# The mean of squares of a head as four 64x64 products, half of the squares made by GpSimd

## The reference

```
def rmsnorm(x, g):
    y = x32 * lax.rsqrt(jnp.mean(x32 * x32, axis=-1, keepdims=True) + NORM_EPS)
    return y * g

q = rmsnorm(split_heads(q, NSA_HEADS), q_g)          # HEAD_DIM = 64
o_slc = nsa_selected(q, rmsnorm(ks, k_g[1]), vs, importance)
o_win = nsa_window(q, rmsnorm(kw, k_g[2]), vw)
q = rmsnorm(split_heads(q, FOX_HEADS), q_g)          # in fox_group
k = rmsnorm(split_heads(k, FOX_HEADS), k_g)
```

## Time and profile before

| | |
|---|---|
| median of 3 runs | 443.76 us (443.74 to 444.36) |
| profiled execution, its own time | 444.42 us |
| its span | 442.5 us |
| granted clock of PE, mean over the span | 0.992 |
| PE, DVE, ACT, POOL busy | 96%, 66%, 59%, 18% of the span |
| chain that ended last, by engine | PE 81%, DVE 10%, ACT 4% |

### The profile page before, as it was taken

The page is one execution under the profiler, slowest core; times in us unless marked ns, Lnnn a source line. Parts: engine busy times, 40 slices in busy tenths (PEclk is TensorE's granted clock), DMA queues, the critical chain, the costliest instruction groups (busy, mean ns, idle before and its releaser), DMA issues.

```text
span 442.5 us, 6412 instructions
## 1 busy us (share of the span) xinstructions
PE 425.2 (96%) x2173; PEld 327.7 (74%) x2173; DVE 291.8 (66%) x609; ACT 262.6 (59%) x510; POOL 78.7 (18%) x129
## 2 busy tenths in 40 slices
PE   5799999999989899999999999999799999999997
PEld 1477788778978666676777987978577678888875
DVE  5976698867798877676158846788977268522204
ACT  4736885766776888877268878742687454311100
POOL 3302420000000275666000010000365200000000
PEclk9899999999999999999999999999899999999999
DMA  7831342342142200000012233642300014722005
GB/s 248 343 101 49 114 126 83 100 115 95 49 142 60 85 1 2 2 1 1 1 48 96 95 96 118 169 142 76 116 1 1 1 48 154 277 101 87 0 0 192
DMA packets 12961, 39.15 MB, mean 88 GB/s; under 512 B 1792, under 2 KB 2048, under 8 KB 12672
## 3 DMA queue, kind: packets, MB, share of 16 engines
q1 hardware_dynamic: 12928, 38.73, 26.8%
HBM read 32.43 MB, written 2.10 MB: 78 GB/s over the span
## 4 chain that ended last, share of the span: by engine, by line
PE 81%; DVE 10%; ACT 4%; issue 3%; DMA 2%; SPq 1%; POOL 0%; DVEq 0%; ACTq 0%
PE bank L1255 11%; PE bank L1257 11%; PE bank L1256 11%; PE bank L1369 7%; PE bank L1350 6%; PE bank L1470 5%; PE bank L1471 5%; PE bank L1469 5%; PE bank L1341 3%; PE bank L1342 3%; PE bank L1266 2%; PE bank L1236 2%; PE bank L1238 2%; PE bank L1237 2%; DMA x_raw<-in_xT 2%
## 5 line engine op out<-in xcount | busy, mean ns | idle before, releaser
L1255 PE MATMUL bank<-xh,wh 128*128 128x512 f32 x256 | 108.4, 423 | 0.3 <-DVE wl L883 0.3
L1257 PE MATMUL bank<-xh,wl 128*128 128x512 f32 x256 | 100.9, 394 | 0.0
L1256 PE MATMUL bank<-xl,wh 128*128 128x512 f32 x256 | 100.2, 391 | 0.0
L883 DVE TENSOR_TENSOR wl<-raw,wh 128x1024 fp32r<-128x1024 f32 (+1 forms) x51 | 61.2, 1204 | 34.7 <-ACT wh L551 34.4
L551 ACT ACTIVATE wh<-raw 128x1024 fp32r<-128x1024 f32 (+1 forms) x51 | 52.3, 1037 | 30.6 <-PE bank L1471 26.8
L1255 PEld LDWEIGHTS bank<-xh,wh 128*128 128x128 f32 x256 | 48.5, 189 | 14.0 <-issue 4.9
L1256 PEld LDWEIGHTS bank<-xl,wh 128*128 128x128 f32 x256 | 48.3, 189 | 13.6 <-issue 3.9
L1257 PEld LDWEIGHTS bank<-xh,wl 128*128 128x128 f32 x256 | 48.3, 188 | 10.9
L1078 DVE CUSTOM_DVE_ANT_0 bank<-bank,mask_row 128x256 f32<-128x256 f32 (+3 forms) x96 | 46.8, 500 | 13.6 <-PE bank L1342 13.0
L511 POOL TENSOR_SCALAR probs<-probs,rcp,gates 128x384 f32<-128x384 f32 (+3 forms) x44 | 27.2, 629 | 103.3 <-DVE rcp L1094 103.3
L1471 PE MATMUL bank<-wh,yl 128*128 128x512 f32 x96 | 37.8, 394 | 0.0
(11 more groups left out here) (213 smaller groups left out, 783.6 us busy)
## 6 DMA issues: line engine op xcount, KB each, us to landing
raw<-in_w_in SPq DMA_DIRECT2D x36, 512.0 KB, 3.3
raw<-in_w_out SPq DMA_DIRECT2D x12, 512.0 KB, 3.3
x_raw<-in_xT SPq DMA_DIRECT2D x8, 256.0 KB, 6.1
x_res<-in_x_tok SPq DMA_DIRECT2D x1, 2048.0 KB, 10.4
out_y<-y_out SPq DMA_DIRECT2D x8, 256.0 KB, 2.1
raw<-in_w_in SPq DMA_DIRECT2D x3, 384.0 KB, 3.1
cmp_w_sb<-in_cmp_w SPq DMA_DIRECT2D x1, 1024.0 KB, 10.1
kh_fox<-kh_fox SPq DMA_DIRECT2D x8, 128.0 KB, 2.3
```

The lines of the kernel that those rows point to most:

```text
L883: dve.tensor_tensor(wl[:, c % HL, cols], raw[:, c % RAW, cols], wh[:, c % HL, cols].bitcast(F32), ALU.subtract).then_inc(wl_ready, 1)
L1255: pe.matmul(dst, hi, xh[:, k, :], start=(k == 0), stop=False)
L1256: pe.matmul(dst, hi, xl[:, k, :], start=False, stop=False)
L1257: mm = pe.matmul(dst, lo, xh[:, k, :], start=False, stop=(k == KT - 1))
```

## The change

Each head mean is now four matmuls of 64 partitions by 64 result rows and 256 tokens, instead of one of 128 by 128 and 512 tokens. Tokens 0 to 255 use the two diagonal blocks. For tokens 256 to 511 the squares of a head lie on the other half of the partitions, so that their products use the two off-diagonal quarters of the array, and their results land on the head's own half again. These late squares are made by POOL (`swapped_squares`, two instructions of 64x256, from one half of the partitions to the other), ACT squares the early half only. Results of early tokens go to bank 4, of late tokens to bank 5 (`HEAD_MEAN`, quarters 0 and 3 of the two banks, which are now one tensor), and `NORM_W` has quarters 1 and 2. Since both banks are now written by the head mean, PE waits for the earlier chunk's `normed`, no longer for `norm_seed`, and for both POOL squares. POOL's program has the squares of `ks` to `nq` 3 before the probabilities of the first attention, those of `fq` 0 to `fk` 3 behind them, and the last `scale_input` between `fk` 0 and `fk` 1.

```diff
--- before.py
+++ after.py
@@ -191,10 +191,14 @@
             x_res = sb("x_res", [P, NT, D], F32, v)
             y_out = sb("y_out", [P, NT, D], F32, v)
 
-        bank = [ctx.enter_context(nc.psum_tensor(f"bank{i}", [P, SEQ], F32)) for i in range(8)]
+        banks = [ctx.enter_context(nc.psum_tensor(f"bank{i}", [P, SEQ], F32)) for i in range(4)]
+        norm_banks = ctx.enter_context(nc.psum_tensor("norm_banks", [P, 2 * SEQ], F32))
+        bank = ([b[:, :] for b in banks] + [norm_banks[:, 0:SEQ], norm_banks[:, SEQ:2 * SEQ]]
+                + [ctx.enter_context(nc.psum_tensor(f"bank{i}", [P, SEQ], F32))[:, :] for i in (6, 7)])
         PROJ = (bank[6], bank[0], bank[1])
         AUX_A, AUX_B, MEAN = bank[2], bank[3], bank[4]
-        NORM_W = bank[5]
+        quarters = norm_banks[:, :].rearrange("p (b c) -> p b c", b=4)
+        HEAD_MEAN, NORM_W = quarters[:, 0::3, :], quarters[:, 1:3, :]
         SCORE = (bank[4], bank[5], bank[6], bank[0])
         PT = (bank[7], bank[1])
         PTB = len(PT)
@@ -227,7 +231,7 @@
         cmp_evac, cmp_sq, cmp_mean, cmp_std = sem("cmp_evac"), sem("cmp_sq"), sem("cmp_mean"), sem("cmp_std")
         k_cmp_n, k_cmp_hr, k_cmp_ready = sem("k_cmp_n"), sem("k_cmp_hr"), sem("k_cmp_ready")
         v_cmp_T, v_cmp_ready = sem("v_cmp_T"), sem("v_cmp_ready")
-        sq_ready, norm_mean, norm_seed = sem("sq_ready"), sem("norm_mean"), sem("norm_seed")
+        sq_ready, sq_swapped, norm_mean, norm_seed = sem("sq_ready"), sem("sq_swapped"), sem("norm_mean"), sem("norm_seed")
         normed, h_ready, l_ready, stacked = sem("normed"), sem("h_ready"), sem("l_ready"), sem("stacked")
         cmp_s, cmp_shift, cmp_exp, cmp_p = sem("cmp_s"), sem("cmp_shift"), sem("cmp_exp"), sem("cmp_p")
         cmp_pT, cmp_pT_sb, cmp_o, cmp_o_read = sem("cmp_pT"), sem("cmp_pT_sb"), sem("cmp_o"), sem("cmp_o_read")
@@ -277,6 +281,9 @@
 
         def pool_square(k):
             return (sq, work, std)[POOL_SQUARES.index(k)][:, :]
+
+        def early_late(ap):
+            return ap.rearrange("p (b c) -> p b c", b=2)
 
         def half_of(s):
             return slice(s * HD, (s + 1) * HD)
@@ -523,14 +530,32 @@
                 pool.wait_ge(lru_ix, j + 1)
                 nc.gpsimd.tensor_tensor(ig[j][:, :], ig[j][:, :], u_pad[j][:, 0:SEQ], ALU.mult).then_inc(lru_ixs, 1)
 
+            def swapped_squares(c):
+
+                n = nth_normed(c)
+                pool.wait_ge(proj_read, proj_units(c) + 1)
+                if n >= 1:
+                    pool.wait_ge(norm_mean, n)
+                for s in range(2):
+                    x = qr[half_of(s), n % 2, SEQ // 2:]
+                    nc.gpsimd.tensor_tensor(sq[half_of(1 - s), SEQ // 2:], x, x, ALU.mult).then_inc(sq_swapped, 1)
+                pool.wait_ge(sq_swapped, 2 * n + 2)
+
             for j in range(LRU_T - 1):
                 gate_input(j)
             for j in range(LRU_T - 1):
                 scale_input(j)
             gate_input(LRU_T - 1)
-            pool.wait_ge(gates_ready, 1)
-            scale_probs(0, NSA_UNITS)
-            scale_input(LRU_T - 1)
+            pool.wait_ge(lru_ix, LRU_T)
+            for c in NORMED:
+                if c == AT["fq", 0]:
+                    pool.wait_ge(gates_ready, 1)
+                    scale_probs(0, NSA_UNITS)
+                    pool.wait_ge(p_scaled, NSA_UNITS)
+                if c == AT["fk", 1]:
+                    scale_input(LRU_T - 1)
+                    pool.wait_ge(lru_ixs, LRU_T)
+                swapped_squares(c)
             scale_probs(NSA_UNITS, UNITS)
 
 
@@ -582,7 +607,7 @@
                     n = nth_normed(c)
                     if n >= 1:
                         act.wait_ge(norm_mean, n)
-                    act.activation(sq[:, :], qr[:, n % 2, :], ACT.Square).then_inc(sq_ready, 1)
+                    act.activation(sq[:, 0:SEQ // 2], qr[:, n % 2, 0:SEQ // 2], ACT.Square).then_inc(sq_ready, 1)
 
             def after(c):
 
@@ -607,8 +632,8 @@
                     eighth = kind in ("nq", "fq")
                     if n >= 1:
                         act.wait_ge(normed, n)
-                    rsqrt_seed(MEAN[:, :], 64.0 if eighth else 1.0, std[:, :], work[:, :],
-                               NORM_W[:, :]).then_inc(norm_seed, 1)
+                    rsqrt_seed(HEAD_MEAN, 64.0 if eighth else 1.0, early_late(std[:, :]), early_late(work[:, :]),
+                               NORM_W).then_inc(norm_seed, 1)
 
             def norm_high(c):
 
@@ -899,7 +924,8 @@
                 if c in NORMED:
                     n = nth_normed(c)
                     dve.wait_ge(norm_seed, n + 1)
-                    link(dve.tensor_tensor(work[:, :], work[:, :], NORM_W[:, :], ALU.mult))
+                    w = early_late(work[:, :])
+                    link(dve.tensor_tensor(w, w, NORM_W, ALU.mult))
                     link(dve.scalar_tensor_tensor(std[:, :], work[:, :], 1.5, std[:, :], ALU.add, ALU.mult))
                     dve.scalar_tensor_tensor(qr[:, n % 2, :], qr[:, n % 2, :], ch(GAIN[kind]), std[:, :], ALU.mult,
                                              ALU.mult).then_inc(normed, 1)
@@ -1261,9 +1287,15 @@
 
                 n = nth_normed(c)
                 pe.wait_ge(sq_ready, n + 1)
+                pe.wait_ge(sq_swapped, 2 * n + 2)
                 if n >= 1:
-                    pe.wait_ge(norm_seed, n)
-                pe.matmul(MEAN[:, :], block_mean, sq[:, :], start=True, stop=True).then_inc(norm_mean, 1)
+                    pe.wait_ge(normed, n)
+                for b in range(2):
+                    for s in range(2):
+                        rows, dst = half_of(s), half_of(s if b == 0 else 1 - s)
+                        mm = pe.matmul(HEAD_MEAN[dst, b, :], block_mean[rows, rows], early_late(sq[:, :])[rows, b, :],
+                                       start=True, stop=True)
+                mm.then_inc(norm_mean, 1)
 
             def gates_of(j):
                 pe.wait_ge(conv_done, j + 1)
```

## The result

| | before | after |
|---|---|---|
| median | 443.75 us (443.21 to 444.36, 6 runs) | 448.69 us (447.13 to 451.43, 6 runs) |
| ratio, 95% interval | | 1.0107 (1.0085 to 1.0129) |
| profiled execution, its own time | 444.42 us | 451.43 us |
| its span, mean granted clock | 442.5 us, 0.992 | 449.4 us, 0.987 |

The change makes the kernel 4.9 us slower, where 3.25 were forecast. The profiled execution is the slowest of its six, so places are read from it and totals from the medians. In the kernel with the change the names move: L885 is the evacuation (L860 before), L908 the split of weights (L883), L928 to L930 the normalisation (L902 to L904), L541 POOL's squares, L1281 to L1283 the projection, L1296 the head mean.

What follows compares the result with a forecast made beforehand. PE, with 81% of the chain, was taken to bound the kernel. Products -1.4, `ks` +1.75, `fk` 1 +1.3, `fk` 0 and `fk` 3 +1.0, `nq` 3 +0.1, others +0.5: +3.25, median 447.0 us, between 444.7 and 449.9.

Steps and rivals of the forecast that it cites:

- The products: Fourteen head means on PE: each costs 0.69 to 0.80 us in place of 0.85, gaining 0.10 per call, -1.4 us together.
- Rival 1: At the head means: products of the two row halves do not run together, about 455 us; chance 1 in 10.
- rival 3: At the head means: shape changes for free when four quarters load together, 442.4 us; counted in 13 in 100 with rival 2.
- POOL's squares: On POOL: one half-width square takes 0.63 us, two 1.25, handovers about 0.1; hidden unless POOL and DVE hold each other up.
- The lock: POOL and DVE hold each other up: whoever starts first has its whole instruction; the other waits.
- `ks` and `fk` 1: L883 right behind the evacuation holds POOL's squares up, so PE waits: +1.75 us at `ks`, +1.3 at `fk` 1.
- if DVE's next instruction gets in between: At `ks`: DVE's next instruction runs between POOL's two squares, making PE's wait +1.95 us in place of +1.6.
- rival 2: Tiling pays and POOL's squares are hidden: 443.96 us, or 441.6 at best; 13 in 100 together with rival 3.
- `fk` 0, `fk` 3, `nq` 3 and the others: PE's waits on `normed`: +1.0 us at `fk` 0 and `fk` 3, +0.1 at `nq` 3, +0.5 at the other nine.
- the lower of my two cases: At `fk` 0 and `fk` 3: wait 0.3 us if POOL and DVE alternate, 0.7 if POOL runs both squares first.
- DVE's lost time makes the weights late: DVE loses 0.1 to 0.5 us in most chunks, costed at nothing; late weights in every chunk would prove the prediction wrong.

Runs made afterwards that it cites:

- dve_yields: The change, but at `ks`, `fq` 0 and `fk` 1 DVE splits the weights only after POOL's two squares; 446.01 us, ratio 1.0054 to the kernel before.
- ks_once: The kernel before, but at `ks` alone POOL makes the late squares in two instructions on the same halves, product whole; 446.93 us, ratio 1.0051.
- ks_twice: The kernel before, but at `ks` alone POOL makes the pair of late squares twice, product whole; 449.29 us, ratio 1.0113.
- warm: The change plus eight useless matmuls on PE ahead of its wait at `ks`; 448.18 us, ratio 1.0101 to the kernel before.
- after_again: The change itself, unaltered, measured once more against the kernel before; 449.15 us, ratio 1.0122.
- w_sbuf_pool: The change, but `NORM_W` kept in SBUF, so PE waits for `norm_seed` and not `normed`; 450.96 us, ratio 1.0157 to the kernel before.
- act_all: The change, but ACT makes all late squares and POOL none; 443.96 us, ratio 1.0003 to the kernel before.
- act_three: The change, but ACT makes the late squares at `ks`, `fq` 0 and `fk` 1; 446.07 us, ratio 1.0049 to the kernel before.
- pool_half: The kernel before, but POOL squares tokens 256 to 511 in one instruction on the same partitions, product whole; 445.14 us, ratio 1.0024.
- best: The change with all squares by ACT, `NORM_W` in SBUF, PE waiting for `norm_seed`, whole square and product at `ks` and `fk` 1; 442.70 us, ratio 0.9989.

## Why the prediction was right, and where not

**The products.** Right in mechanism, a little too high in gain. The step without a wait was 0.70, at the lower end of 0.69 to 0.80; with the 0.09 of getting in, which my range was to hold, it is 0.79, at the upper. The gain per head mean is 0.07 for the 0.10 taken, and -1.0 for -1.4. Rival 1 (the row halves do not run together, 1.1 to 1.2) and rival 3 (the shape changes for free, under 0.5) both fell. 0.79 - 0.43 = 0.36 us go for the change of shape, near the 0.37 of the earlier trace rows.

**POOL's squares.** 0.61 for the 0.63 taken. The handover from DVE was 0.15 in place of 0.05, and that from DVE's `normed` to PE 0.15 in place of 0.06, for which no row was shown. The lock did what the earlier trace rows said.

**`ks` and `fk` 1.** Right, and each 0.2 us too small. At `ks` the case "if DVE's next instruction gets in between", priced 1.95, is what happened and what was measured, and I had taken the mean of both cases. At `fk` 1 it is 1.5, the upper end of my range, with the longer handovers. dve_yields shows the cause and rules out rival 2, in which L883 would not hold POOL up.

**`fk` 0, `fk` 3, `nq` 3 and the others.** `normed` came 5.92 us behind the head mean before and 6.0 to 6.2 after, since the engines alternate; at `fk` 0 and `fk` 3 this is the lower of my two cases, and I had taken the middle: 0.3 for 1.0. Less was given back behind `nq` 3 (0.3) than I took. `nq` 0 and `nq` 2 waited 0.28 each. These errors nearly cancel: 1.25 for 1.6. The instructions of the normalisation became less slow than I said: L930 0.12 us on average and 0.24 at most, for 0.3 to 0.5.

**What the sum lacked.** With these terms the sum is +3.7, 0.45 above the forecast: that they come so near is in part luck, since the products and `fk` 0 and `fk` 3 erred the other way. Two costs have no term. One the prediction names and puts at nothing: DVE's lost time makes the weights late, not in every chunk but in front of two value chunks, 0.7 us in the trace. The other is PE's clock, 0.9 us by the estimate above, and 1.4 in the profiled execution. The stop at `ks` was priced at its own length. What it does to the matmuls behind it was not asked, although this stop is longer than any that the kernel before has in the stretches of the head means (1.04 us), and although the trace of the kernel before shows half clock behind its own two stops of 2.0 us. That the stop brings the half clock on is shown by ks_once and ks_twice, in which it appears with nothing but the stop added, and by ks_twice's time; warm and dve_yields, whose one trace each has no half clock there, agree. In the change it does not follow in every execution.

**What stays open.** Of five traces with a stop of 2.1 us or more at `ks` (after, after_again, ks_once, ks_twice, w_sbuf_pool) four show the half clock behind it; none of those with 0.4 to 1.2 does (warm, act_all, act_three, dve_yields, pool_half). Elsewhere it is alike: all thirteen traces have a stop of 2.0 near 316 us with half clock beginning in it or right behind; near 16 us nine have a stop of 1.8 to 2.0, seven of them with half clock behind it (not warm and best), and the four with at most 1.2 have none. Why three stops of this length bring none, why the stop of 1.6 at `fk` 1 had none, and why none follows the 4.5 us that PE stands at the start of every span, the runs don't tell. How much of w_sbuf_pool's extra 2 us is the clock was not separated; its one execution at a clock of 0.996 took 448.81 us, where the change's three at that clock took 447.1 to 447.6.

## What to carry to other kernels

Work that is moved to an idle engine must be ready before the bound engine comes, and the two slow each other down when GpSimd and VectorE both read two SBUF operands: look at what VectorE starts right behind the handover, and at which operand sits in PSUM. A split of an instruction into tiles that run side by side pays only for what is left over the change of shape, here 0.07 of 0.86 us. A stop of PE can cost more than its length: read the granted clock behind every long stop that the trace of the kernel before has, and price a new one by it.

## What the runs showed of the hardware

- Behind a stop of 2.1 to 3.9 us at `ks` PE ran at half clock for some 3 us, in four of five traces; after 2.2 us of stop it lost a further 1.45 us. In the thirteen traces PE stood 1.8 us or more 27 times after its first matmul; at 24 of them half clock began in the stop or within some 2 us behind it.
- GpSimd's square of 64x256 and that of 128x256 took the same 1.46 us beside the same VectorE instruction (64 or 128 partitions make no difference), and 0.61 us alone.
- Four 64x64 products of 256 columns, each in two passes, took 0.70 us and 0.09 to get in, against 0.85 to 0.86 for one of 128x128 and 512 columns.
- ScalarE wrote squares to the opposite half of the partitions in 0.42 us for 64x256, less than GpSimd's 0.61, and nothing held it up.
